# Retention's norms for four heads at once, token squares moved over a 32-column table, and the keys' weights split earlier

## What is computed

```python
y_ret = retention_chunkwise(rq, rk, rv)
y_ret = y_ret * lax.rsqrt(jnp.mean(y_ret * y_ret, axis=-1, keepdims=True) + EPS)
y_ret = from_heads(y_ret) * ret_norm_g[layer].astype(jnp.float32)
y_ret = (jax.nn.silu(r_g.astype(jnp.float32)) * y_ret).astype(x.dtype) @ w_ret_out[layer]
```

## Time and profile before

| | |
|---|---|
| time, median of three runs | 1568.97 us |
| the profiled execution, its own time | 1569.27 us |
| its span in the profile | 1567.4 us |
| TensorE busy | 1546.3 us (99%) |
| VectorE busy | 985.7 us (63%) |
| ScalarE busy | 790.6 us (50%) |
| GpSimd busy | 577.4 us (37%) |
| DMA, mean over the span | 160 GB/s |

### The profile page before, as it was taken

The page is one execution under the profiler, slowest core; times in us unless marked ns, Lnnn a source line. Parts: engine busy times, 40 slices in busy tenths (PEclk is TensorE's granted clock), DMA queues, the critical chain, the costliest instruction groups (busy, mean ns, idle before and its releaser), DMA issues.

```text
span 1567.4 us, 20288 instructions
## 1 busy us (share of the span) xinstructions
PE 1546.3 (99%) x7624; PEld 1266.4 (81%) x7624; DVE 985.7 (63%) x1226; ACT 790.6 (50%) x926; POOL 577.4 (37%) x248
## 2 busy tenths in 40 slices
PE   9999999999999999999999999999999999999998
PEld 7888788887888888888889868767888888888886
DVE  6366231492465799999877489764554574656556
ACT  5265223434245788888865161694334453424344
POOL 1422363433442222322222836344332335252524
PEclk9999999999999999999999999999999999999999
DMA  5421242222237899999966324401420405050511
GB/s 207 128 74 54 84 146 86 81 81 80 85 109 296 322 421 417 385 387 391 385 269 232 113 84 135 122 1 58 158 81 29 160 27 188 28 188 27 176 53 54
DMA packets 49192, 250.89 MB, mean 160 GB/s; under 512 B 9888, under 2 KB 12704, under 8 KB 22880
## 3 DMA queue, kind: packets, MB, share of 16 engines
q1 hardware_dynamic: 42480, 236.59, 41.1%
q0 software_dynamic: 5184, 8.40, 1.5%
q10 hardware_dynamic: 1456, 4.92, 0.8%
HBM read 234.27 MB, written 16.78 MB: 160 GB/s over the span
## 4 chain that ended last, share of the span: by engine, by line
PE 83%; issue 6%; DVE 4%; POOL 4%; ACT 2%; DMA 1%; SPq 0%; ACTq 0%; POOLq 0%; DVEq 0%
PE psum L232 23%; PE psum L234 23%; PE psum L233 23%; POOL w_both L148 3%; PE psum L703 2%; PE psum L2466 2%; PE psum L2501 1%; PE psum L1437 1%; PE psum L2489 1%; PE psum L705 1%; ACT w_both L142 1%; PE psum L724 1%; PE psum L2790 1%; PE psum L2386 1%; PE psum L761 1%
## 5 line engine op out<-in xcount | busy, mean ns | idle before, releaser
L148 POOL TENSOR_TENSOR w_both<-raw,w_both 128x2048 fp32r<-128x2048 f32 x62 | 289.1, 4664 | 456.1 <-ACT w_both L142 421.1
L232 PE MATMUL psum<-x_hi,w_both 128*128 128x512 f32 (+1 forms) x624 | 243.6, 390 | 4.8 <-POOL w_both L148 4.8
L1455 DVE TENSOR_TENSOR moe_lo<-moe_w,moe_hi 128x2048 fp32r<-128x2048 f32 x100 | 228.3, 2292 | 31.4 <-ACT moe_hi L1445 30.2
L233 PE MATMUL psum<-x_lo,w_both 128*128 128x512 f32 (+1 forms) x624 | 240.8, 386 | 0.0
L234 PE MATMUL psum<-x_hi,w_both 128*128 128x512 f32 (+1 forms) x624 | 240.8, 386 | 0.0
L142 ACT ACTIVATE w_both<-raw 128x2048 fp32r<-128x2048 f32 x67 | 128.0, 1911 | 203.9 <-PE psum L234 201.9
L1445 ACT ACTIVATE moe_hi<-moe_w 128x2048 fp32r<-128x2048 f32 x100 | 191.5, 1916 | 27.9 <-PE psum L234 21.9
L2918 POOL TENSOR_TENSOR unit_lo<-mlp_raw,unit_hi 128x2048 fp32r<-128x2048 f32 x24 | 111.1, 4630 | 180.1 <-ACT unit_hi L2913 102.4
L232 PEld LDWEIGHTS psum<-x_hi,w_both 128*128 128x128 f32 x624 | 118.0, 189 | 30.6 <-issue 7.7
L233 PEld LDWEIGHTS psum<-x_lo,w_both 128*128 128x128 f32 x624 | 117.9, 189 | 23.5 <-issue 0.7
L234 PEld LDWEIGHTS psum<-x_hi,w_both 128*128 128x128 f32 x624 | 117.9, 189 | 23.5
(11 more groups left out here) (450 smaller groups left out, 3343.8 us busy)
## 6 DMA issues: line engine op xcount, KB each, us to landing
raw<-in_w_dense SPq DMA_DIRECT2D x67, 1024.0 KB, 4.9
moe_w<-in_w_moe_ahead SPq DMA_DIRECT2D x54, 1024.0 KB, 13.1
moe_w<-in_w_moe SPq DMA_DIRECT2D x48, 1024.0 KB, 12.7
mlp_raw<-in_w_mlp SPq DMA_DIRECT2D x28, 1024.0 KB, 4.9
yrow<-expert_rows SPq DMA_DIRECT2D x8, 512.0 KB, 7.2
res<-in_x SPq DMA_DIRECT2D x4, 512.0 KB, 6.5
hn_rows<-hn_tok ACTq DMA_DIRECT2D x4, 512.0 KB, 5.5
raw<-in_w_dense SPq DMA_DIRECT2D x2, 512.0 KB, 5.5
```

Of the source, the lines that this page charges most:

```text
L148: pool.tensor_tensor(w_lo[c % RING][:, :], raw[c % RING][:, :], w_hi[c % RING][:, :].bitcast(F32), ALU.subtract).then_inc(lo_ready, 1)
L232: pe.matmul(out, lh, rh, start=first, stop=False, **more)
L233: pe.matmul(out, lh, rl, start=False, stop=False, **more)
L1455: dve.tensor_tensor(ring_lo[s][:, :], ring[s][:, :], ring_hi[s % MOE_HI][:, :].bitcast(F32), ALU.subtract).then_inc(moe_low, 1)
```

## The change

**Norms.** `mean_squares(q)` sums the squares of four heads, in float32, with a table of 32 columns of ones, each head's into its own 32 rows of one bank. ScalarE takes one root and VectorE one reciprocal for the four heads. `factors_spread(q)` spreads one row of each over 128 rows, into banks 4 to 7, and `retention_norm` multiplies with it from there. The first quad is summed right behind the values, the second within the first `ret_g` tile; the spreads stand behind tile 0 and tile 2. GpSimd's splits and the two-pass form go.

**Token squares.** In `token_sums` the squares move and the gains' table, now 2 x 16 columns, is stationary; features `kt` and `kt + 4` are added in one of four groups of 32 rows. The sums, with tokens along the row, are copied to SBUF by ScalarE and brought to the tokens' partitions by four small matmuls over a table that adds the four groups (`sums_by_token`). `token_sums(1)` moves behind the first half tile of `keys`, and the turning of the wide table behind the last.

**Keys' weights.** The chunk for `keys` is loaded ahead of the rows. Its parts go to 144 and 152, the room of the value weights, as soon as these are used: the high part on ScalarE behind two value tiles, the low part on VectorE ahead of the first `both`.

```diff
+    def mean_squares(pe, q):
+        pe.wait_ge(rsq_done, 4 * q + 4)
+        for g in range(4):
+            mm = pe.matmul(psum[32 * g:32 * g + 32, quad_bank(q), :], ones[:, 0:32], ret_sq[4 * q + g][:, :],
+                           start=True, stop=True)
+        mm.then_inc(quad_summed, 1)
+    def factors_spread(pe, q):
+        pe.wait_ge(ri_done, 4 * q + 4)
+        if q:
+            pe.wait_ge(ry_done, 4)
+        for g in range(4):
+            mm = pe.matmul(psum[:, 4 + g, :], ones[32 * g:32 * g + 1, :], ret_rms[q][32 * g:32 * g + 1, :],
+                           start=True, stop=True)
+            mm.then_inc(rm_done, 1)
+    def quad_inverted(dve, q):
+        dve.wait_ge(rr_done, 4 * q + 4)
+        dve.reciprocal(ret_rms[q][:, :], ret_rms[q][:, :]).then_inc(ri_done, 4)
     def retention_norm(dve, h):
-        dve.wait_ge(rr_done, h + 1)
-        dve.reciprocal(ret_rms[h][:, :], ret_rms[h][:, :]).then_inc(ri_done, 1)
-        dve.wait_ge(ri_done, h + 1)
+        dve.wait_ge(rm_done, h + 1)
         dve.scalar_tensor_tensor(out=ret_y[:, h, :], in0=ret_y[:, h, :], scalar=col("ret", h),
-                                 in1=ret_rms[h][:, :], op0=ALU.mult, op1=ALU.mult).then_inc(ry_done, 1)
+                                 in1=psum[:, 4 + h % 4, :], op0=ALU.mult, op1=ALU.mult).then_inc(ry_done, 1)
...
-            if t + 2 < HEADS:
-                retention_norm(dve, t + 2)
+            if t == 0:
+                for h in (1, 2, 3):
+                    retention_norm(dve, h)
+                quad_inverted(dve, 1)
+            if t == 2:
+                for h in (4, 5, 6, 7):
+                    retention_norm(dve, h)
...
-        pe.wait_ge(rr_done, 1)
-        dense_pe(pe, "ret_g", x_hi, x_lo,
-                 tile_hooks={0: lambda: [mean_square(pe, h) for h in range(3, HEADS)] + [pe.wait_ge(rr_done, 2)],
-                             1: lambda: pe.wait_ge(rr_done, 3), 2: lambda: pe.wait_ge(rr_done, 4)})
+        dense_pe(pe, "ret_g", x_hi, x_lo, step_hooks={6: lambda: mean_squares(pe, 1)},
+                 tile_hooks={0: lambda: [factors_spread(pe, 0), pe.wait_ge(rr_done, 4)],
+                             2: lambda: [factors_spread(pe, 1), pe.wait_ge(rr_done, 8)]})
...
     def combine_sync(sp):
+        load_chunk(sp, FIRST_CHUNK["keys"])
         for q in range(TB):
             for k in range(2):
                 sp.dma_start(yrow[k][q][:, :], expert_rows[k * S + q * P:k * S + (q + 1) * P, :])\
                   .then_inc(yrows_landed[q], 16)
-            if q >= 2:
-                load_chunk(sp, FIRST_CHUNK["keys"] + q - 2)
+        load_chunk(sp, FIRST_CHUNK["keys"] + 1)
...
+        keys_low(dve)
         both(0)
...
-        split_lo(dve, FIRST_CHUNK["keys"])
...
-        for j in range(3):
+        for j in range(2):
             v_mem_out(j)
+        keys_high(act)
+        v_mem_out(2)
         gated(0)
...
-            mm = pe.matmul(psum[:, 5, P * q:P * q + P], esq[q % 2][:, kt, :],
-                           gw[:, kt, :, :].rearrange("p s n -> p (s n)"), start=(kt == 0 and q == 0),
-                           stop=(kt == KT - 1), skip_group_check=True)
+            g = NR_WIDE * (kt % 4)
+            mm = pe.matmul(psum[g:g + NR_WIDE, 5, P * q:P * q + P], gw[:, kt, :, :].rearrange("p s n -> p (s n)"),
+                           esq[q % 2][:, kt, :], start=(kt < 4 and q == 0), stop=(kt >= 4), tile_position=(0, g),
+                           skip_group_check=True)
         mm.then_inc(esum_sq, 1)
+    def sums_by_token(pe):
+        pe.wait_ge(tok_steps, TOK_COPIED)
+        for q in range(TB):
+            mm = pe.matmul(psum[:, 4, 2 * q:2 * q + 2], sums_t[:, q * P:(q + 1) * P], picks[:, 0:NR_WIDE:NR_WIDE // 2],
+                           start=(q == 0), stop=(q == TB - 1), skip_group_check=True)
+        mm.then_inc(tok_steps, 1)
...
         keys(0, 0)
+        token_sums(pe, 1)
         keys(1, 0)
         token_sums(pe, 2)
         token_sums(pe, 3)
         pe.wait_ge(xq_low, TB)
         keys(0, 1)
+        sums_by_token(pe)
+        keys(1, 1)
         pe.wait_ge(tok_steps, TOK_WIDE)
         for n in range(2 * TB):
             mm = pe.transpose(psum[:, 7 - n // TB, (n % TB) * P:(n % TB + 1) * P], end_wide[:, n, :], ident[:, :])
         mm.then_inc(tok_steps, 1)
-        keys(1, 1)
```

More of the change, by code:

```diff
@@ L1033, in build @@
     ret_y = at("ret_y", 80, [P, KT, S])
-    SQUARES_KB = (134.5, 136.5, 108, 106, 134.5, 136.5, 108, 110)
-    SPLIT_HEADS = 5
+    SQUARES_KB = (134.5, 136.5, 108, 106, 100, 102, 104, 110)
     ret_sq = [at(f"ret_sq{h}", kb, [P, S]) for h, kb in enumerate(SQUARES_KB)]
-    ret_rms = [at(f"ret_rms{h}", 96 + 2 * h, [P, S]) for h in range(HEADS)]
+    ret_rms = [at(f"ret_rms{q}", kb, [P, S]) for q, kb in enumerate((96, 108))]
     tables_landed, TABLES_BEFORE = first_landed, 16
@@ L1043, in build @@
                                   "normed"))
[L1044 to L1047, removed]
+    quad_summed, QUADS_BEFORE = s_high, HEADS
     RET_T = FIRST_TILE["ret_g"]
@@ L1110, in retention_tensor @@
         values(2)
-        mean_square(pe, 0)
-        mean_square(pe, 1)
         values(3)
[L1114 to L1136, removed]
+        mean_squares(pe, 0)
@@ L1190, in squared, with rooted @@
         def squared(h):
-            if h in (4, 5, 6):
-                act.wait_ge(rm_done, h - 3)
             act.activation(ret_sq[h][:, :], psum[:, value_bank(h), :], ACT.Square).then_inc(rsq_done, 1)
[L1195 to L1198, removed]
+        def rooted(q):
+            act.wait_ge(quad_summed, QUADS_BEFORE + q + 1)
+            act.activation(ret_rms[q][:, :], psum[:, quad_bank(q), :], ACT.Sqrt, scale=1.0 / RV,
+                           bias=col("eps")).then_inc(rr_done, 4)
         norm_mem.warm_up(act)
-        for h in range(4):
+        for h in range(6):
             copied(h)
             squared(h)
[L1203 to L1208, removed]
         copied(6)
         copied(7)
+        rooted(0)
         squared(6)
         squared(7)
-        for h in range(2, HEADS):
-            rooted(h)
+        rooted(1)
     g_tmp = [at(f"g_tmp{b}", 144 + 2 * b, [P, S]) for b in range(4)]
@@ L1946, in build, with keys_high, keys_low @@
     tok_r12 = end_r[:, 0:TB]
+    keys_hi, keys_lo = (at(f"keys_{n}", 144 + 8 * i, [P, CHUNK_COLS], FR) for i, n in enumerate(("hi", "lo")))
+    def keys_high(act):
+        c = FIRST_CHUNK["keys"]
+        act.wait_ge(v_done, 2)
+        act.wait_ge(raw_landed[c % RING], 16 * (c // RING + 1))
+        act.activation(keys_hi[:, :], raw[c % RING][:, :], ACT.Copy).then_inc(hi_ready, 1)
+    def keys_low(dve):
+        c = FIRST_CHUNK["keys"]
+        dve.wait_ge(v_done, 4)
+        dve.wait_ge(hi_ready, c + 1)
+        dve.tensor_tensor(keys_lo[:, :], raw[c % RING][:, :], keys_hi[:, :].bitcast(F32), ALU.subtract)\
+           .then_inc(lo_ready, 1)
     def combine_sync(sp):
+        load_chunk(sp, FIRST_CHUNK["keys"])
         for q in range(TB):
@@ L2001, in combine_vector @@
         low(3)
-        dve.wait_ge(esum_sq, TB)
-        s0, s1 = (psum[:, 5, :].rearrange("p (q s n) -> p s q n", s=2, n=HD)[:, i, :, 0] for i in range(2))
+        dve.wait_ge(tok_steps, TOK_SUMMED)
+        s0, s1 = (psum[:, 4, 0:2 * TB].rearrange("p (q s) -> p s q", s=2)[:, i, :] for i in range(2))
         link(dve, dve.tensor_scalar(end_eps[:, :], s0, EPS / D, EPS * EPS, ALU.mult, ALU.add))
@@ L2342, in keys @@
         def keys(m, half):
-            slot = KEYS_C % RING
-            wh = w_hi[slot][:, :].rearrange("p (m k n) -> p m k n", k=KT, n=P)
-            wl = w_lo[slot][:, :].rearrange("p (m k n) -> p m k n", k=KT, n=P)
+            wh, wl = (t[:, :].rearrange("p (m k n) -> p m k n", k=KT, n=P) for t in (keys_hi, keys_lo))
             n = slice(2 * P * half, 2 * P * half + 2 * P)
```

25 lines of the change are left out of this document (15 added, 10 removed).

## The result

The changed kernel took 1560.04 us (median of five runs, 1559.75 to 1561.29); the kernel before, on the same chip, 1568.97 (five runs, 1568.56 to 1571.67). The ratio is 0.9939, with a 95% interval of 0.9927 to 0.9951, so it is faster by about 9 us. The forecast was 1561.0. The profiled execution took 1560.04 us with a span of 1558.2.

The account below looks back on a forecast made before the run. TensorE was taken to bound the kernel, busy 1546.3 of 1567.4 us. From 1569.27, +0.1 (norms), -6.35 (wait near 370) and -2.0 (end of layer one) gave 1561.0 us; own range 1558.0 to 1564.2, with two rivals 1558.0 to 1566.0.

Parts of the forecast that it names:

- Norm groups, +0.1: Retention's norms on TensorE: four groups of 1.4 us, 5.6 in all, replace 5.53 us; net +0.1, from -1.1 to +2.1.
- rival (a): Retention's norms: the one-row spreads go one after the other, price 4.6 us, 1565.6 us; chance 0.09.
- The wait near 370, -6.35: TensorE's wait for GpSimd's low half (L148) goes whole, with the slow clock behind it: -6.35 us, with 3.5 to spare.
- (b): The gate's wait stays because ScalarE's squares and table load, not VectorE, hold the high half; 1567.4 us, chance 0.06.
- (d): Retention groups and token sums: narrow forms don't overlap at all; +4.0 us, 1573.3, slower; chance 0.04.
- eight squares of the memory and a table load, to about 358: ScalarE's work behind its last high part (about 352), ahead of two sigmoids and the late chunk's high half.
- The new wait, 1.2: End of layer one: TensorE waits 1.2 us before value tile 4 for ScalarE's copy, queued behind the keys' chunk; no lower clock.
- rival (c): The keys' chunk lands 2.4 us later; TensorE stands 3.6 us before value tile 4, slow clock after; 1566.0 us, chance 0.07.
- Start of keys, -2.0: End of layer one: keys(0, 0) wants only token_sums(0) and low(1), so it starts at 838.7 instead of 840.66, 2.0 us earlier.
- From there to q_idx, no change (15.96): TensorE from keys(0, 0): half tiles 11.66, token sums 1.0 and 1.6, sums_by_token 0.9, transposes 0.8; 15.96 us against 16.0 now.
- Rival (e): Keys' weights are split sooner but nothing waits for them, since low(1) sets the start; already in the sum, no chance given.

Follow-up runs that it names:

- six_recips: The kernel after with six unused 128x512 reciprocals put back on VectorE, one per gate tile from the third to the last; 1566.12 us, ratio 0.9978.
- one_recip: The kernel after with one unused 128x512 reciprocal more on VectorE, ahead of the last low part of retention's gated output; 1564.81 us, ratio 0.9974.
- copy_first: The kernel after with the copy of value tile 2 ahead of the keys' high half on ScalarE; 1560.45 us, ratio 0.9947.
- sums_back: The kernel after with token_sums(1) put back ahead of the first half tile of keys; 1560.01 us, ratio 0.9943.
- late_keys: The kernel after with the keys' chunk loaded, split and placed as before, its low half on VectorE behind the two `low`; 1563.35 us, ratio 0.9962.
- norms_only: The kernel before with only the part of the change on retention's norms; 1563.25 us, ratio 0.9962.
- one_row_group: The kernel after with four more one-row float32 matmuls, all from row 0, ahead of each of the two spreads; 1572.22 us, ratio 1.0021.

## Why the prediction was right, and where it was wrong

**Norm groups, +0.1.** They gave -0.7 (4.84 for 5.53). Four side by side was right for both kinds, rival (a) is out. The term that was too large is entering and leaving the form: 0.55 was put down, and 0.25 to 0.41 is left (1.11 to 1.27 less 0.86). The row that spoke for the one-row spreads was weaker than it was taken for: the records of L724 have 512, 384, 256 and 128 columns, so their mean of 0.21 us doesn't show two side by side all through. That four one-row calls overlap rested on the likeness to 32 columns alone.

**The wait near 370, -6.35.** Right: 7.0 for the norms less the 0.7 of the groups is 6.3, the wait is gone with its slow clock, and six_recips shows the chain from VectorE's reciprocals. Rivals (b) and (d) are out. The cover was misjudged. The step "eight squares of the memory and a table load, to about 358" took them to run through, but they wait for VectorE, whose `y_lo` are held beside GpSimd. They ended at 360.9, the slack is 0.84 and not 3.5, and one_recip shows that 3.3 us more uses it up. The trace of before had the sign of it, a `y_lo` of 4.68 us at 318.79. The time came out as forecast all the same, since 0.84 is still more than nothing; so much of it was luck.

**The new wait, 1.2.** Right in place and size: 1.28 of the lead, 1.1 of it idle. The chunk's split began at 813.7 (the forecast had it landing at 820.1, with a lead of 6.5 us), its cause is the one named, and no lower clock followed, so rival (c) is out. The forecast had the second rows arrive just in time for the delayed transposes; what it did not draw from this is that they hold the transposes by about the same amount once the wait is gone (copy_first).

**Start of keys, -2.0.** Right: 832.18 against 840.66 is 8.48, less the lead of 6.48 is 2.00. It starts when `low(1)` ends, as forecast (829.77 and 2.35 are 832.12), but the move of `token_sums(1)`, named with it, has no part in it (sums_back).

**From there to q_idx, no change (15.96).** It took 15.25 (832.18 to 847.43) against 16.01, so 0.76 came on top. The mis-sized term is the token sums: 0.57 and 1.01 where 1.0 and 1.6 were put down. The 16 records come to 0.035 each with what entering the form costs in it; in the trace the waves of four start 0.109 apart, 0.027 a record, just the pace of four side by side that the forecast had worked out and then did not trust: it put down 0.6 for them and 0.4 for the form. The four half tiles took 12.1 instead of 11.66, since each stands behind a change of form: in the trace the first step of the second one is 0.22, where the steps within it are 0.12. By the page "TensorE: Matmul & The Clock Gate" of the Trainium skill (Step-by-step: what each phase is for), a matmul decoded in firmware takes about 62 ns. Here the trace doesn't agree: a record takes 27 to 35 ns, and a call of two records 55 in the waves. The Trainium skill gives this figure for one of two ways of decoding, and no trace shows which one runs here.

**Rival (e), "the early split gives by itself at most the 2.0 and costs the 1.2".** Wrong in size: late_keys is 3.3 us slower than the kernel after. The step took `low(1)` to set the start of `keys` either way. But the chunk's low half stands behind `low(1)` on VectorE, and with the token sums short and one of them moved, nothing of TensorE's lies over it any more. It stands for over 3 us, and half clock follows. Without the early split this place gives nothing (late_keys against norms_only), and the move of `token_sums(1)`, which the forecast counted among its reasons, gives nothing (sums_back).

**The sum.** 1569.27 - 0.7 - 6.3 - 2.8 is 1559.5, and 0.13 lost at the start and 0.39 in the loop make 1560.0. The forecast was 1 us high because the price of the narrow forms was too high twice, by 0.8 and 0.76, less these 0.5, which it did not have.

## What to carry to other kernels

Small matmuls that use a quarter of the array belong side by side, in four row or column groups, and back to back: four float32 calls of 512 columns then cost 1.1 to 1.3 us and eight of 128 columns 0.6, and in a single group about three times that; for one-row operands the clock fell as well. When a late buffer is traced back over three engines, look for the piece of each chain that is held by another engine before you call the rest slack. When an edit takes work from under which a transfer or a split was hidden, ask what that work had covered; here the short sums gave nothing without the early split.

## What the runs showed of the hardware

- The granted clock fell to 0.50 while TensorE was busy without a gap, during one-row matmuls in one row group (2.4 us of them, one_row_group), and stayed there for 10.2 us, more than half of it under full products. Four row groups with the same one-row operands did not bring it down, but they last only 1.1 us; a longer run of them was not tried.
- A wait of 2.27 us left the clock at 1.00 in the one trace that shows it (one_recip); waits of 2.85, 3.27 and 3.60 us were followed by 0.50 (six_recips, late_keys, before).
- Float32 records of 512 columns take 0.43 us and those of 128 columns 0.109 in one group of the array; four groups side by side bring the latter to 0.035 with entering the form, 0.027 without.
- A VectorE operation on two SBUF inputs was drawn out from 0.7 to 4.7 us beside a GpSimd operation of 4.6, and to 2.5 beside one of 2.4; one with an input in PSUM took its usual 0.69.
